# Forgetting attention: the short meta-key groups of both heads transposed together, their value products on 64 rows of the array

## What is computed

```python
def forgetting_attention(q, k, v, log_f):
    # softmax(q k^T / sqrt(d) + c_t - c_s) v over s <= t, c = cumsum(log f); 8 heads of 64
    def block(inp):
        q_b, c_b, start = inp
        logits = (jnp.einsum('bqhd,bkhd->bhqk', q_b, kf)
                  + c_b[..., None] - c_k[:, :, None, :])
        logits = jnp.where(key_pos[None, :] <= q_pos[:, None], logits, -jnp.inf)
        return jnp.einsum('bhqk,bkhd->bqhd', jax.nn.softmax(logits, axis=-1), vf)
```

## Time and profile before

| | |
|---|---|
| median of 3 runs | 2209.12 us (2207.74 to 2210.43) |
| the profiled execution, its own time | 2208.28 us |
| its span, first to last instruction | 2206.7 us |
| granted TensorE clock, mean over the span | 0.999 |
| TensorE matmuls busy | 2180.8 us, 99% of the span |
| VectorE / ScalarE / GpSimd busy | 1426.9 us (65%) / 1074.4 us (49%) / 149.0 us (7%) |
| the 240 attention transposes (L1799) | 36.8 us busy |
| the value products (L1823), 448 records of 128 columns | 29.6 us busy |

### The profile page before, as it was taken

How to read it: one execution, slowest core, us unless ns; L and a number is a source line. 1 busy time by engine, 2 the same in 40 slices (tenths; PEclk the granted TensorE clock), 3 DMA queues, 4 the chain that set the end, 5 groups by cost and what they waited for, 6 DMA issues and landing times.

```text
span 2206.7 us, 39505 instructions
## 1 busy us (share of the span) xinstructions
PE 2180.8 (99%) x15687; PEld 1999.4 (91%) x15687; DVE 1426.9 (65%) x2673; ACT 1074.4 (49%) x2045; POOL 149.0 (7%) x245
## 2 busy tenths in 40 slices
PE   9999999999999999999999999999999999999998
PEld 8799999999997899999899889978899888998997
DVE  5356699559744466897498566869444465863664
ACT  5356656347533465555377534223344444552652
POOL 4111010100000011100000010101000000000001
PEclk9999999999999999999999999999999999999999
DMA  6666678885335546674355263767521222543651
GB/s 212 194 173 161 187 195 237 230 242 179 129 108 156 162 116 167 190 194 146 124 175 159 81 187 102 210 194 214 148 68 67 67 96 86 158 159 118 183 174 51
DMA packets 106434, 341.92 MB, mean 155 GB/s; under 512 B 15126, under 2 KB 19196, under 8 KB 103692
## 3 DMA queue, kind: packets, MB, share of 16 engines
q1 hardware_dynamic: 91900, 228.87, 31.6%
q0 software_dynamic: 13632, 109.23, 21.4%
q10 hardware_dynamic: 720, 1.31, 0.2%
HBM read 337.23 MB, written 106.99 MB: 201 GB/s over the span
## 4 chain that ended last, share of the span: by engine, by line
PE 88%; DVE 6%; ACT 3%; issue 2%; POOL 1%; POOLq 0%; ACTq 0%; DVEq 0%
PE G L1486 52%; PE G L1523 17%; PE G L1602 7%; PE X L1523 3%; DVE wL L2500 2%; PE X L1823 1%; PE X L1910 1%; PE X L1775 1%; PE X L1799 1%; ACT wH L1963 1%; PE X L1894 1%; PE X L1879 1%; PE X L1562 1%; PE X L1866 0%; PE X L1729 0%
## 5 line engine op out<-in xcount | busy, mean ns | idle before, releaser
L1963 ACT ACTIVATE wH<-raw 128x512 fp32r<-128x512 f32 (+3 forms) x751 | 495.8, 681 | 431.0 <-PE G L1486 348.0
L2500 DVE TENSOR_TENSOR wL<-raw,wH 128x512 fp32r<-128x512 f32 (+3 forms) x751 | 561.2, 760 | 216.5 <-ACT wH L1963 213.3
L1486 PE MATMUL G<-aH,wH 128*128 128x264 f32 (+3 forms) x1680 | 432.3, 319 | 2.0 <-DVE aL L2513 1.2
L1486 PE MATMUL G<-aH,wL 128*128 128x264 f32 (+3 forms) x1680 | 413.9, 308 | 0.0
L1486 PE MATMUL G<-aL,wH 128*128 128x264 f32 (+3 forms) x1680 | 413.9, 308 | 0.0
L1486 PEld LDWEIGHTS G<-aH,wH 128*128 128x128 f32 (+1 forms) x1680 | 273.6, 188 | 22.2 <-issue 2.1
L1486 PEld LDWEIGHTS G<-aH,wL 128*128 128x128 f32 (+1 forms) x1680 | 271.7, 187 | 16.3
L1486 PEld LDWEIGHTS G<-aL,wH 128*128 128x128 f32 (+1 forms) x1680 | 271.9, 188 | 13.0 <-issue 0.2
L1523 PE MATMUL G<-seven,wH 128*128 128x256 f32 (+2 forms) x1200 | 220.7, 283 | 6.2 <-issue 3.4
L1523 PEld LDWEIGHTS G<-seven,wH 128*128 128x128 f32 x1200 | 184.4, 188 | 9.0 <-issue 6.6
L2661 DVE TENSOR_TENSOR hT<-G,hT 128x528 f32<-128x528 f32 (+1 forms) x83 | 58.0, 699 | 201.2 <-PE G L1486 201.0
(11 more groups left out here) (412 smaller groups left out, 3979.7 us busy)
## 6 DMA issues: line engine op xcount, KB each, us to landing
raw<-weights SPq DMA_DIRECT2D x175, 512.0 KB, 4.2
raw<-weight_sums SPq DMA_DIRECT2D x200, 256.0 KB, 3.0
weight_sums<-weights POOLq DMA_DIRECT2D x72, 704.0 KB, 6.4
raw<-weights SPq DMA_DIRECT2D x151, 256.0 KB, 3.0
raw<-weights SPq DMA_DIRECT2D x48, 704.0 KB, 4.2
weight_sums<-weight_sums POOLq DMA_DIRECT2D x24, 704.0 KB, 4.6
weight_sums<-weights POOLq DMA_DIRECT2D x24, 640.0 KB, 6.9
weight_sums<-weights POOLq DMA_DIRECT2D x24, 448.0 KB, 5.0
```

The costliest lines, as they stand in the source:

```text
L1486: done = e.matmul(m.pair(i)[0:M, bank, 0:n], a[:, k, 0:M], b[:, kx, lo - t0:lo - t0 + n], start=(k == 0 and c == 0), stop=(k == nk - 1 and ...
L1963: e.activation(m.high(i)[:, c], m.raw(i)[:, c], ACT.Copy).then_inc(s.w_hi, 1)
L2500: e.tensor_tensor(m.low(i)[:, c], m.raw(i)[:, c], m.high(i)[:, c].bitcast(F32), ALU.subtract).then_inc(s.w_lo, 1)
```

## The change

It has six parts.

1. **Tiles.** VectorE writes the normalised weights of the 16 meta keys no longer into `Sb` but into a new tile `pfox`, both heads side by side (and in kind 0 both query groups, 32 columns apart). One transpose then serves the meta keys of both heads; in kind 0 one more serves the meta queries of both. `fox_tiles(u)` has 8, 7 and 9 tiles: 2, 2 and 3 rounds. The shared tiles come last.
2. **Products.** The products with the meta keys read 64 rows of `PT` (0 to 63 for head 0, 64 to 127 for head 1), so their stationary tiles are 64 rows by 64 columns. All others keep 128 rows. `fox_products(u)` gives the order: `(i, 1), (i, 0), (i, 2), ...` for each query group, and `(0, -1)` at the end of kind 0. The number of products stays.
3. **Values.** `fvmeta`, new, on ScalarE: three copies of 16x512 per layer put the meta values where those 64 rows expect them (`fv` rows 64 to 79, and a new tile `fv2`).
4. **VectorE.** The multiplies of `Sb` leave out the meta columns; one, and in kind 0 three, small multiplies per head into `pfox` follow them and raise `f_pmeta`, for which a unit's last round waits.
5. **POOL.** `zeros` also clears `pfox` (128x384) and `fv2` (128x512) ahead of `kzero`.
6. **Order.** The second half of `nsum` gets a turn of its own behind the rounds. Kind 0 of the first pair has one `yield` less.

```diff
 def fox_tiles(u):
+    out = [(hh, i, j, at + TOK[j][0]) for hh in range(2) for i, at in FOX[u % 3] for j in range(1, i + 1)]
+    return out + [(1, 0, 0, 0)] + [(1, 0, -1, 144)] * (u % 3 == 0)
+
+def fox_products(u):
     out = []
-    for hh in range(2):
-        for i, at in FOX[u % 3]:
-            out += [(hh, i, -1, 144)] * (i == 1) + [(hh, i, j, at + TOK[j][0]) for j in range(i + 1)]
-    return out
+    for i, _ in FOX[u % 3]:
+        out += [(i, 1), (i, 0)] + [(i, j) for j in range(2, i + 1)]
+    return out + [(0, -1)] * (u % 3 == 0)
+
+def fox_meta_row(u, hh, i, j):
+    return 32 * (2 * hh + i - 1) if u % 3 == 0 and j == 0 else 64 * hh
...
                 for r in range(fox_rounds(u) if u < 12 else 0):
                     step("ft", l, u, r)
-                    if kind == 0 and p and r == 2:
-                        step("nsum", l, p - 1, 1)
+                    last_query()
+                    yield
+                if u < 12 and kind == 0 and p:
+                    step("nsum", l, p - 1, 1)
                     last_query()
                     yield
...
     def ft(l, u, r):
+        if tiles[-1][2] <= 0:
+            e.wait_ge(s.f_pmeta, 2 * (12 * l + u) + 2)
+        for q, (hh, _, j, at) in enumerate(tiles):
+            source = m.Sb[:, fox_row(u) + hh, at:at + 128] if j > 0 else m.pfox[:, u % 2 if j == 0 else 2, :]
+            done = e.transpose(X[:, 2 + r % 2, 128 * q:128 * q + 128], source, m.ident[:, :])
...
     def fo(l, u):
+        for i, j in products:
             for hh in range(2):
                 c = 128 * p + 64 * hh
-                done = e.matmul(X[64 * hh:64 * hh + 64, 3, at:at + nq], m.fv[:, max(j, 0), c:c + 64],
-                                m.PT[:, one * hh + q, 0:nq], start=(j <= 0), stop=(j < 0 or j == i))
+                t = slot[hh, i, j] if j > 0 else slot[1, 0, j]
+                r = slice(0, 128) if j > 0 else slice(64 * hh, 64 * hh + 64)
+                values = m.fv[r, j, c:c + 64] if j > 0 else m.fv2[r, c:c + 64] if (i, j) == (2, 0) else m.fv[r, 0, c:c + 64]
+                done = e.matmul(X[64 * hh:64 * hh + 64, 3, at:at + nq], values, m.PT[r, t, 0:nq],
+                                start=(j == 1 or j < 0), stop=(j < 0 or (j == i > 1) or (j == 0 and i == 1)))
...
+    def fvmeta(l, t):
+        e.wait_ge(s.tm_meta, TM_NTH["fv", l])
+        out = m.fv[64:80, 0, :] if t == 2 else m.fv2[32 * t:32 * t + NM, :]
+        e.activation(out, m.fv[0:16, 0, :], ACT.Copy).then_inc(s.fvmeta, 1)
...
     def fn(l, u, hh):
-        main = row[:, 0:TOK[FOX[kind][0][0]][0] + 128]
+        main = row[:, NM:TOK[FOX[kind][0][0]][0] + 128]
...
-            e.tensor_scalar(row[0:16, 144:160], row[0:16, 144:160], sc[0:16, 6:7], None, ALU.mult).then_inc(*own.one())
-            e.tensor_scalar(row[:, 160:432], row[:, 160:432], sc[:, 9:10], None, ALU.mult).then_inc(*own.one())
+            e.tensor_scalar(row[:, 176:432], row[:, 176:432], sc[:, 9:10], None, ALU.mult).then_inc(*own.one())
         e.tensor_scalar(main, main, sc[:, 3:4], None, ALU.mult).then_inc(s.f_norm, 1)
+        if kind == 0:
+            e.tensor_scalar(m.pfox[0:16, 2, 64 * hh:64 * hh + NM], row[0:16, 144:160], sc[0:16, 6:7], None,
+                            ALU.mult).then_inc(*own.one())
+            at = fox_meta_row(u, hh, 2, 0)
+            e.tensor_scalar(m.pfox[:, u % 2, at:at + NM], row[:, 160:176], sc[:, 9:10], None, ALU.mult).then_inc(*own.one())
+        at = fox_meta_row(u, hh, 1, 0)
+        e.tensor_scalar(m.pfox[:, u % 2, at:at + NM], row[:, 0:NM], sc[:, 3:4], None, ALU.mult).then_inc(s.f_pmeta, 1)
...
     def zeros(l):
+        constant(m.pfox[:, :, :], 0.0)
+        constant(m.fv2[:, :], 0.0)
         ordered()
         e.memset(m.fv[:, 0, :], 0.0).then_inc(s.kzero, 1)
```

More of the change, by code:

```diff
@@ L629, in fg @@
             yield from tm()
-            for _ in range(4):
+            for n in range(4):
                 yield from fm()
+                if n:
+                    step("fvmeta", l, n)
             for role in ("gr", 0), ("gr", 1), ("fk", 2), ("fq", 2), ("gr", 2), ("gr", 3), ("fk", 3), ("fq", 3):
@@ L1159, in __init__ @@
         self.sigm, self.go_sq, self.gn_ln, self.gn_exp = new("sigm"), new("go_sq"), new("gn_ln"), new("gn_exp")
-        self.f_exp, self.f_pt, self.f_out = new("f_exp"), new("f_pt"), new("f_out")
+        self.f_exp, self.f_pt, self.f_out, self.fvmeta = new("f_exp"), new("f_pt"), new("f_out"), new("fvmeta")
         self.nsq, self.n_ln, self.n_exp, self.fsum_ln = new("nsq"), new("n_ln"), new("n_exp"), new("fsum_ln")
@@ L1177, in __init__ @@
         self.fsum, self.f_max, self.f_norm, self.mix_fox = new("fsum"), new("f_max"), new("f_norm"), new("mix_fox")
-        self.f_meta = new("f_meta")
+        self.f_meta, self.f_pmeta = new("f_meta"), new("f_pmeta")
         self.taps, self.gated, self.hid_lo = new("taps"), new("gated"), new("hid_lo")
@@ L1267, in __init__ @@
                 self.wau = sb("wau", [113, 256], F32, cf)
+                self.pfox = sb("pfox", [128, 3, 128], F32, cf)
+                self.fv2 = sb("fv2", [128, 512], F32, cf)
         with ExitStack() as c:
@@ L1797, in ft @@
             e.wait_ge(s.f_pt, t - 1)
-        for q, (hh, _, _, at) in enumerate(tiles):
-            done = e.transpose(X[:, 2 + r % 2, 128 * q:128 * q + 128], m.Sb[:, fox_row(u) + hh, at:at + 128], m.ident[:, :])
+        if tiles[-1][2] <= 0:
[3 more added lines that the diff above has]
+            done = e.transpose(X[:, 2 + r % 2, 128 * q:128 * q + 128], source, m.ident[:, :])
         done.then_inc(s.ft, 1)
@@ L1808, in fo @@
             e.wait_ge(s.tm_meta, TM_NTH["fv", l])
+            e.wait_ge(s.fvmeta, 3 * l + 3)
             e.wait_ge(s.gn_ln, 4 * l + 4)
@@ L1815, in fo @@
         tiles = fox_tiles(u)
-        one = len(tiles) // 2
-        for q in range(one):
-            _, i, j, _ = tiles[q]
+        slot = {(hh, i, j): q for q, (hh, i, j, _) in enumerate(tiles)}
+        products = fox_products(u)
+        for i, j in products:
             at = 0 if j < 0 or kind else TOK[i][0]
@@ L1822, in fo @@
                 c = 128 * p + 64 * hh
-                done = e.matmul(X[64 * hh:64 * hh + 64, 3, at:at + nq], m.fv[:, max(j, 0), c:c + 64],
-                                m.PT[:, one * hh + q, 0:nq], start=(j <= 0), stop=(j < 0 or j == i))
-                if q == one - 1:
+                t = slot[hh, i, j] if j > 0 else slot[1, 0, j]
[3 more added lines that the diff above has]
+                                start=(j == 1 or j < 0), stop=(j < 0 or (j == i > 1) or (j == 0 and i == 1)))
+                if (i, j) == products[-1]:
                     done.then_inc(s.fo, 1)
@@ L2437, in act_program @@
              "go": go, "gn": gn, "fsum": fsum, "ft": ft, "fs": fs, "fo": fo, "nsq": nsq, "nsum": nsum, "is": iscore, "dt": dt,
-             "ds": ds, "do": do}
+             "ds": ds, "do": do, "fvmeta": fvmeta}
     for kind, *args in STEPS:
@@ L3177, in zeros @@
         constant(m.glrT[64:128, :], 1.0)
+        ordered()
+        constant(m.pfox[:, :, :], 0.0)
+        constant(m.fv2[:, :], 0.0)
         ordered()
```

6 lines of the change are left out of this document (added).

## The result

| | before | after |
|---|---|---|
| median | 2209.11 us (2207.74 to 2210.43, 4 runs) | 2225.08 us (2225.03 to 2226.62, 4 runs) |
| the profiled execution, its own time | 2208.28 us | 2225.05 us |
| its span | 2206.7 us | 2223.8 us |

The ratio is 1.0073, with a 95% interval of 1.0061 to 1.0085: 16.0 us or 0.7% slower. The forecast was 0.46% slower at 2219.2 us; the measured time lies inside its range, near the upper end.

The account below looks back on a forecast made before the run. TensorE, busy 99% of the span, was taken as the bound. −5.3 + 10.1 + 6.1 − 0.8 = +10.1 us on 2208.28 gives 2218.4; with 0.84 for the median, 2219.2 us, 0.46% slower; range 2210.5 to 2226.5.

Parts of the forecast that it names:

- rival (c): Value products: two row tiles writing one PSUM bank take turns, 3.5 to 7 us more, 2222.7 to 2226.2 us; chance 0.15.
- Transposes: 48 fewer, −5.3 us: TensorE's queue in both layers' attention: 192 transposes instead of 240, at 0.11 us each, all taken in full.
- Products: … 72 more changes of tile shape, +10.1 us: Value products on TensorE: same number, 9 new inner shape changes a pair, 72 in all, at 0.14 us each.
- The first round now waits for head 1, +6.1 us: Kinds 0 and 1: first round waits for head 1's `f_norm`; 1.4, 0.4, 0.4, 1.1 us, +3.1 a layer.
- the line for being wrong here: Sign for the first-round waits: wrong on this second point if the waits for VectorE sum to under 3 us.
- Waits behind the rounds, −0.8 us: Unit 0's third-round wait gone, −1.6 us; `fo` waits 0.4 us a layer, +0.8; the `nsum` waits' sum left unchanged.
- At nothing: Costed at zero: six `fvmeta` copies on ScalarE (3.6 us without cover) and two POOL memsets, about 0.53 us each.
- (a): Change of rows free: without the waits 2203.8 us, faster, chance 0.05; with the waits 2209.1, no change, chance 0.08.
- (b): Drain as forecast, waits absorbed: +4.8 us, 2213.9 us; with half the waits 2216.5; chance of 2213.9's neighbourhood 0.15.
- (d): Value products: row tiling pays, 64-row passes of both heads at half cost, 3.5 us back, 2215.7 us; chance 0.05.

Follow-up runs that it names:

- e5_all: Changed kernel with all products on 128 rows (masked meta values), rounds by head in the earlier turns, and new memsets behind `kzero`'s; 2205.95 us, 0.9980 of the kernel before.
- e1_shapes: Changed kernel with its value products reordered, 32 instead of 72 inner changes of tile shape; 2221.81 us, 1.0054 of the kernel before.
- e2_rows128: Changed kernel with all value products on 128 rows, meta values zero in the other head's columns; 2215.20 us, 1.0030 of the kernel before.
- e6_before_both: Kernel before with one wait changed: the first round of kinds 0 and 1 waits for both heads' `f_norm`; 2211.58 us, 1.0012 of the kernel before.
- e3_pool: Changed kernel with the two new POOL memsets behind the one that raises `kzero`, with their own semaphore; 2226.35 us, 1.0078 of the kernel before.
- e8_all2: Changed kernel's own rounds, with 128-row products, memsets behind, and two k-steps more in pair 0 of each layer; 2216.31 us, 1.0034 of the kernel before.
- e4_heads: Changed kernel with rounds that keep the heads apart and `nsum`'s second half again directly behind the third round; 2218.01 us, 1.0039 of the kernel before.

## Why the prediction was right, and where not

The side held, and so did the range, the range in part by luck: its upper end of 2226.5 stood there for rival (c), which is not what happens. The sum was +10.1 us and the measured difference is +16.0; on the profiled executions +16.8. Step by step:

- **"Transposes: 48 fewer, −5.3 us"**: held. 192 are left. Added up from the start of each transpose to the start of the next matmul, without waits, they take 8.4 us a layer instead of 11.0, 2.5 less for the forecast's 2.65. e5_all, where almost nothing else remains, is 3.5 us under the kernel before at the third mark, in spite of two waits.
- **"Products: … 72 more changes of tile shape, +10.1 us"**: held, +10.4 measured. The row I took, 16x64 next to 64x64, gave 0.14 for a change from 128x64 to 64x64, and it is 0.149 beside the same order in one shape. The new place of the 16-column product, which the sum left out, gives 0.3 us back. e1_shapes and e2_rows128, with 32 changes and none for 72, show that the cost goes with the number of changes, and e1_shapes that it does not go with the number of 64-row passes.
- **"The first round now waits for head 1, +6.1 us"**: right mechanism, somewhat too large. By the brackets 1.26, 0.07, 0.07 and 0.81 us came, 2.2 a layer. The forecast's 0.4, 0.4 and 1.1 were worked out from start to start, and so counted 1.42, 0.23, 0.23 and 0.97 came, 2.85 us a layer where 0.37 was before: +2.5 for the forecast's +3.1, or 5.0 us for 6.1. I had left VectorE's own gain out: the 16x16 multiply no longer stands ahead of head 1's main one, which ends 0.15 us sooner behind the scores. Put into the kernel before by itself, the wait costs 3.7 us (e6_before_both), since part of it only takes the place of the waits behind it. A layer's 2.2 us by the brackets is under the 3 us that I had set as the line for being wrong here; counted from the starts it is just under too.
- **"Waits behind the rounds, −0.8 us"**: this is the step that failed. Unit 0's third round is indeed gone with its 0.82. For `fo` I allowed 0.4 us a layer and 1.05 came (0.52, 0.12, 0.41), and two waits were not in my sum at all: 0.86 us for the logarithm at unit 3's second round and 0.89 for `aL` at 220 us. I had followed each wait to the operation it names, and not to what that operation is queued behind. By the brackets a layer has 5.7 us of waits for 1.7 before, and 2.2 of them, with the 0.52 at unit 0's `fo`, were where I had put them. The stretches give what they cost in full: 8.3 = 5.2 (products) − 2.65 (transposes) + 5.7 more waiting. Of these 5.7 us the brackets hold 4.0. Another 1.1 are what the brackets leave out at twelve waits instead of four (0.16 us each, at `fo` 0.07), and 0.6 I can't place. Less the 2.5 us of the first rounds, 3.2 us a layer or 6.4 in all came where this term had −0.8.
- **"At nothing"**: in the trace nothing waits for the copies of `fvmeta`, and in the second layer TensorE has no wait between 640 us and the last matmul on `glrT`, so there the memsets cost nothing, as said. The first layer's memsets cost 1.0 us on the trace (e3_pool). I had checked one reader of `kzero` and not VectorE's.

The rivals: (a) is excluded by e2_rows128, in both of its cases. (b) goes the wrong way; the waits grew. (c) would have given the measured time, and is not why: had I read the total alone, I would have confirmed it. By (c) the products would have cost 3.5 to 7 us beyond the changes of shape, and e1_shapes would have kept that; the changes alone account for all of it (0.148 us each in unit 4 of e1_shapes, with one change and both 64-row passes). The starts of the two heads' 64-row passes in unit 4, both writing bank 3, are 183.153 and 183.160, 7 ns apart, and the 128-row couples in bank 3 start 7 ns apart as well. The gotcha of the Trainium skill, "TensorEngine Tiling (Array Packing)", Restrictions and Gotchas, does not show where the two tiles have different columns too. (d) is wrong as well: behind a change the second pass starts 0.160 us after the first, with 64 rows (183.153 to 183.313) as with 128 (183.519 to 183.679), and the earlier trace rows have the same 0.109 a pass for 64 rows in one shape. The Trainium skill, "TensorEngine Tiling (Array Packing)", Theoretical Speedup, gives up to twofold for a contraction of 64 or less; here nothing of it came. The two heads already lay side by side by columns, and no more products ran at once than before.

## What to carry to other kernels

Before some matmuls are made smaller, count how often the shape of the tile then changes in the queue: here one change cost more than a whole pass (0.149 us for 0.109), and masking the unused rows with zeros was 10 us cheaper than skipping them. For each wait that an edit moves, read the queue of the engine that releases it: a copy behind an activation that itself waits for VectorE is late by both. When a rearrangement saves work but joins two producers in one round, try it with the rounds cut so that each still needs one producer where that can be had; that brought 0.7% slower down to 0.4%, and together with masked products and the later memsets it came to 0.2% faster. And when a wait's price matters, read it from start to start and not from the gap that the profile prints.

## What the runs showed of the hardware

- A change between 128x64 and 64x64 tiles costs 0.149 us (e2_rows128 beside the change, 72 changes). In unit 4 some 0.1 us of it lies at the change (0.206 and 0.220 from start to start for 0.109) and 0.05 at the second pass behind it (0.160 for 0.109). The Trainium skill, "TensorEngine Tiling (Array Packing)", Key Properties, says that a change of tiling mode drains TensorE; the cost at this couple agrees with that.
- Two 64x64 tiles on different rows and different columns write one PSUM bank with starts 7 ns apart (183.153 and 183.160).
- The printed gap of a wait is 0.16 us short behind a projection matmul: 1.26 for 1.42 us at 135.68. It is counted from an end 0.28 us behind the start, and the next matmul usually starts 0.12 us behind it.
- In one of ten traces TensorE ran 3.4 us at half clock soon after a pause of 1.97 us (e8_all2, 1018.9 to 1022.3 us); e4_heads had the same pause and kept the full clock.
